# Who makes the low parts of the key/value filler's weights in the layers' attention: GpSimd, or VectorE in pairs

## The chip, the core and the metric

The kernel runs on one core of a Trainium2 chip. The time is device microseconds from start to end of the one launch. The core has TensorE (PE) for matrix products, VectorE (DVE) and ScalarE (ACT) for element work, GpSimd (POOL) for element work and powers, and SyncE (SP), which issues most DMAs. The engines run their own instruction streams and meet by semaphores.

## What is computed

Two transformer layers of one kind, then one block of another, on 256 rows of width 1024. What bears on this change is the attention of the two layers, and a projection of the last block that is computed beside it:

```python
for l in range(DEPTH):                       # DEPTH = 2, the "layers"
    proj = h @ w_in[l]                       # q, k, v of 8 + 8 heads, 2 + 2 key/value heads
    oa = global_attention(qa, ka, va)
    ob = window_sink_attention(qb, kb, vb, sink[l], slopes)
    mix = jnp.concatenate([rms(oa), rms(ob)], axis=-1) @ w_o[l]
    h = layer_norm(ALPHA * h + mix, ...)
    ...                                      # a PEER feed-forward, layer norm
# second block, cross attention:
mn = rmsnorm(mem, norm_mem)                  # depends on inputs alone
kx, vx = jnp.split(mn @ w_kv_x, 2, axis=-1)  # 1024 x 2048 weights
```

`mem` is an input, so `mn @ w_kv_x` can be computed at any time. The kernel does it inside the layers' attention, the keys in layer 0 and the values in layer 1.

## The kernel before

Large products are made in three passes for precision. Each weight is split into a high part `wh` (fp32r, a reduced form of fp32) and a low part `wl = w - wh`, and so are the activations (`xh`, `xl`); the product is xh·wh + xl·wh + xh·wl. Weights come in chunks of 1 MB, `[128, 2048]` fp32, into a ring of two slots (`ring[:, s, :]`). A chunk has four quarters of 128x512. For each quarter ScalarE copies the high part (`high`, L1405, signals `high_ready[q]`), and either GpSimd (`low`, L510) or VectorE (`low`, L2084) subtracts it to make the low part (signals `parts_ready[q]`); then TensorE multiplies, and signals `parts_free[q]`. When the last low part of a chunk is done, `chunk_free[s]` reaches 2, and SyncE issues the load of the next chunk into that slot. SyncE issues strictly in the order in which its program is written.

The attention of a layer is 8 units (a quarter of 8 heads' queries in each of two row tiles; units 0 to 3 are the windowed kind with sink, 4 to 7 the global kind). Per unit, TensorE makes scores, VectorE takes the maximum (`first`, L2160 or L2163 to L2170), ScalarE the exponentials (L1511), TensorE turns the probabilities (L688), ScalarE takes them out of PSUM (L1457), TensorE multiplies by the values (L971), and VectorE divides (`finish`, L2275 to L2294). VectorE's order per unit u is: scores of u + 2, `late(u - 1)`, wait for the values of u, `finish(u)`. `late` (L2301 to L2310) scales finished heads by a power that GpSimd makes (L496) after `finish` asked for it. `own` makes an engine wait for its own last write.

The **filler** is the key/value product: 4 chunks of 4 quarters, 16 quarters, two per unit. TensorE's order in unit u is: scores of u + 2, filler quarter 2u (`kv_quarter`, L1038), turned probabilities of u + 1, filler quarter 2u + 1, values of u. ScalarE makes a pair of high parts per unit 1 to 6 (`kv_high`), for quarters 4 to 15 (the first chunk's are made before the attention), and every second unit takes a finished filler chunk out of PSUM (`kv_done`, L1582) into the buffer `kvo`, which SyncE saves to DRAM (L354); from the second chunk on `kv_done` first waits until the save before it has landed (`kv_saved`), and its end lets TensorE begin the next filler chunk (`kv_free`). The chunks' low parts are GpSimd's (`kv_lows`, L594 to L606): after its rotation of the queries it makes 12 of them in six pairs, with the powers in between. The first chunk's four low parts are made by GpSimd (L566) and VectorE, two each. In SyncE's program the load of the fourth filler chunk stands ahead of the save of the first, and that load waits for slot 1 of the ring.

After the attention TensorE turns `o_all` (`to_xT`, L720) in two row tiles; for the second it waits for VectorE's last scaling. Before that it runs 14 dummy matmuls (L694).

Of the kernel before, what the change touches and what calls it, by code (L numbers as in the profile page):

```python
# [19 lines left out]
QW = CHUNK // 4  # L20
# [22 lines left out]
def build(nc, A, out):  # L43
# [4 lines left out]
    with ctx:  # L48
# [3 lines left out]
        def sem(name):  # L52
            return ctx.enter_context(nc.semaphore(name))
# [142 lines left out]
        mem_in = sem("mem_in")  # L196
        mem_used = sem("mem_used")
        memvar_ready, memrstd_ready = sem("memvar_ready"), sem("memrstd_ready")
        kv_begun = sem("kv_begun")
        kv_full, kv_free = sem("kv_full"), sem("kv_free")  # L200
        kv_out, kv_saved, kv_in = sem("kv_out"), sem("kv_saved"), sem("kv_in")
        memgain_in = sem("memgain_in")
# [269 lines left out]
        def _(pool):  # L472
            def own(ins):
                ins.then_inc(pool_own, 1)
                pool.wait_ge(pool_own, 1)
                pool.sem_inc(pool_own, -1)
# [15 lines left out]
            def power(n, at=0):  # L492

                pool.wait_ge(var_ready, 1)
                pool.sem_inc(var_ready, -1)  # L495
                pool.tensor_tensor(rstd[:, at:at + n], ve[:, at:at + n], mhalf[:, :].to_broadcast([P, n]),  # L496
                                   ALU.pow).then_inc(rstd_ready, 1)
# [8 lines left out]
            def low(s, q, parts=3):  # L506

                pool.wait_ge(high_ready[q], 1)
                pool.sem_inc(high_ready[q], -1)  # L509
                part = pool.tensor_tensor(wl[:, q, :], ring[:, s, q * QW:(q + 1) * QW],  # L510
                                          wh[:, q, :].bitcast(F32), SUB)
                if q < parts - 1:
                    part.then_inc(parts_ready[q], 1)
                else:
                    own(part)
                    pool.sem_inc(parts_ready[q], 1)
                    pool.sem_inc(chunk_free[s], parts - 2)
# [18 lines left out]
            for l in range(DEPTH):  # L536
# [56 lines left out]
                                           .to_broadcast([P, 10, HD]), MUL))  # L593
                pool.sem_inc(rotated_ready, 1)  # L594

                def kv_lows(s, q0):
                    for q in (q0, q0 + 1):
                        pool.wait_ge(high_ready[q], 1)
                        pool.sem_inc(high_ready[q], -1)
                        part = pool.tensor_tensor(wl[:, q, :], ring[:, s, q * QW:(q + 1) * QW],  # L600
                                                  wh[:, q, :].bitcast(F32), SUB)
                        if q < 3:
                            part.then_inc(parts_ready[q], 1)
                        else:
                            own(part)
                            pool.sem_inc(parts_ready[3], 1)  # L606
                            pool.sem_inc(chunk_free[s], 2)

                kv_lows(1, 0)
                pool.wait_ge(kv_begun, 1)  # L610
                pool.sem_inc(kv_begun, -1)
                kv_lows(1, 2)
                kv_lows(0, 0)
                power(16)
                kv_lows(0, 2)
                kv_lows(1, 0)
                power(4, 16)
                power(4, 24)
                kv_lows(1, 2)
                power(4, 20)  # L620
                low(0, 0)
                power(4, 28)
                low(0, 1)
# [1207 lines left out]
        def _(dve):  # L1831
# [248 lines left out]
            def low(s, q, freed=1):  # L2080

                dve.wait_ge(high_ready[q], 1)
                dve.sem_inc(high_ready[q], -1)  # L2083
                part = dve.tensor_tensor(wl[:, q, :], ring[:, s, q * QW:(q + 1) * QW],  # L2084
                                         wh[:, q, :].bitcast(F32), SUB)
                if q < 3:
                    part.then_inc(parts_ready[q], 1)
                else:
                    own(part)
                    dve.sem_inc(parts_ready[3], 1)  # L2090
                    dve.sem_inc(chunk_free[s], freed)
# [28 lines left out]
                                          xh[:, part, t * P:(t + 1) * P].bitcast(F32), SUB  # L2120
                                          ).then_inc(slot_free[2 + t] if i else xl_half[t], 1)

            def attention(units, first, finish, before=None, late=None, second=None):

                def scores(u):
                    s = u % 2
                    dve.wait_ge(dve_full[s], 1)
                    dve.sem_inc(dve_full[s], -1)
                    first(u, s)

                scores(0)
                if before:
                    before()
                scores(1)
                if second:
                    second()
                for u in range(units):
                    if u + 2 < units:
                        scores(u + 2)
                    if late:  # L2140
                        late(u - 1)
                    dve.wait_ge(dve_full[3], 1)
                    dve.sem_inc(dve_full[3], -1)
                    finish(u, 3)
                if late:
                    late(units - 1)
# [39 lines left out]
            for l in range(DEPTH):  # L2186
# [70 lines left out]
                def kv_lows():  # L2257
                    low(0, 2)
                    low(0, 3)
                    dve.sem_inc(kv_begun, 1)  # L2260

                def first(u, s):
                    ab, g, t = 1 - u // 4, u // 2 % 2, u % 2
# [49 lines left out]

                dve.wait_ge(gain_in[2], 16)
                dve.sem_inc(gain_in[2], -16)
                attention(8, first, finish, mem_lows, late, kv_lows)
                dve.sem_inc(gain_free[1], 1)
                halves_low_xT()
                low(0, 3)
# [720 lines left out]
```

## Time and profile before

| | |
|---|---|
| time, median of 3 runs | 2522.37 us (2522.11 to 2525.31) |
| the profiled execution | 2519.75 us, span 2517.1 us |
| TensorE busy | 2411.9 us, 96% |
| VectorE busy | 1747.7 us, 69% |
| ScalarE busy | 1344.4 us, 53% |
| GpSimd busy | 709.3 us, 28% |
| low parts of the filler on GpSimd (L600) | 24, at 83.2 to 1126.9 us |
| attention, layer 0, first scores to last values | about 60 to 129 us |
| attention, layer 1 | about 1069 to 1132 us |

How to read it: the busy times are shares of the whole span and say which engine sets the pace on the whole. What the change is worth must be read in the two attention stages, 5% of the span, from what each engine waits for there. In the rows "idle before <- X" is the time an engine sat idle before the instruction, and what ended it; "POOLq L599" and the like mean the engine's own sequencer, at a wait on that line.

### The profile page before, as it was taken

The page shows a single profiled execution, that of the slowest core. Times are in us where ns is not written, and L with a number is a line of the kernel's source. Part 1 is how long each engine was busy: PE and PEld are TensorE (multiplying, and loading weights), DVE is VectorE, ACT ScalarE, POOL GpSimd, SP SyncE. Part 2 cuts the span into 40 slices and gives each one's busy share as a digit, 9 for nine tenths or more (in the row PEclk, how much of TensorE's full clock was granted, in tenths as well). Part 3 has the DMA queues.
Part 4 walks back from the last instruction along what each step waited for, and adds up shares of the span by engine and source line. Part 5 has one row for each costly group of instructions (what it writes and reads, how often), then busy time and mean ns, then how long its engine had stood idle before and what let it go on. Part 6 is the DMA issues. An engine that isn't in the chain of part 4 may idle for free. (4 is left out here: it accounts for less than half of the span.)

```text
span 2517.1 us, 57290 instructions
## 1 busy us (share of the span) xinstructions
PE 2411.9 (96%) x16475; PEld 2207.7 (88%) x16475; DVE 1747.7 (69%) x3905; ACT 1344.4 (53%) x2396; POOL 709.3 (28%) x564
## 2 busy tenths in 40 slices
PE   7899999999999999989999999999999998899998
PEld 6789999999888888888999999988888887688996
DVE  5647777887777777564777788767777767455346
ACT  3545555776655555454455567655555543344443
POOL 5665444000000000556544400000000053144665
PEclk9999999999999999999999999999999998999999
DMA  6244566444566666624466644556666644433554
GB/s 240 79 156 157 211 221 224 170 160 171 185 236 246 238 241 240 239 79 140 167 210 227 228 164 151 180 176 247 236 243 239 245 156 155 141 134 110 177 183 149
DMA packets 98051, 475.27 MB, mean 189 GB/s; under 512 B 11809, under 2 KB 13345, under 8 KB 50721
## 3 DMA queue, kind: packets, MB, share of 16 engines
q1 hardware_dynamic: 97392, 472.91, 53.0%
q10 hardware_dynamic: 560, 1.19, 0.1%
q8 instruction: 44, 0.72, 0.1%
q14 instruction: 55, 0.44, 0.1%
HBM read 438.41 MB, written 35.65 MB: 188 GB/s over the span
## 5 line engine op out<-in xcount | busy, mean ns | idle before, releaser
L1405 ACT ACTIVATE wh<-ring 128x512 fp32r<-128x512 f32 x1428 | 882.7, 627 | 610.9 <-ACTq L1404 607.7
L2084 DVE TENSOR_TENSOR wl<-ring,wh 128x512 fp32r<-128x512 f32 x961 | 675.4, 708 | 268.4 <-DVEq L2083 250.7
L1093 PE MATMUL PS<-xh,wh 128*128 128x256 f32 x2048 | 593.4, 290 | 8.3 <-PEq L1089 6.3
L1093 PE MATMUL PS<-xl,wh 128*128 128x256 f32 x2048 | 579.2, 283 | 0.0
L1093 PE MATMUL PS<-xh,wl 128*128 128x256 f32 x2048 | 579.0, 283 | 0.0
L510 POOL TENSOR_TENSOR wl<-ring,wh 128x512 fp32r<-128x512 f32 x295 | 392.8, 1353 | 289.9 <-POOLq L509 286.7
L889 PE MATMUL PS<-wh,xh 128*128 128x512 f32 x1088 | 425.1, 391 | 2.3 <-PEq L886 2.1
L889 PE MATMUL PS<-wh,xl 128*128 128x512 f32 x1088 | 423.4, 389 | 0.0
L889 PE MATMUL PS<-wl,xh 128*128 128x512 f32 x1088 | 423.3, 389 | 0.0
L1093 PEld LDWEIGHTS PS<-xh,wh 128*128 128x128 f32 x2048 | 392.0, 191 | 15.3 <-issue 14.7
L1093 PEld LDWEIGHTS PS<-xl,wh 128*128 128x128 f32 x2048 | 392.6, 192 | 0.0
L1093 PEld LDWEIGHTS PS<-xh,wl 128*128 128x128 f32 x2048 | 392.0, 191 | 0.0
L496 POOL TENSOR_TENSOR rstd<-ve,mhalf 128x1 f32<-128x1 f32 (+3 forms) x30 | 30.2, 1007 | 1243.0 <-POOLq L495 1222.9
L636 POOL TENSOR_TENSOR wl<-ring,wh 128x512 fp32r<-128x512 f32 x144 | 205.5, 1429 | 230.3 <-POOLq L635 229.9
L889 PEld LDWEIGHTS PS<-wh,xh 128*128 128x128 f32 x1088 | 204.2, 188 | 48.8 <-issue 6.8
L889 PEld LDWEIGHTS PS<-wh,xl 128*128 128x128 f32 x1088 | 204.2, 188 | 42.8
L889 PEld LDWEIGHTS PS<-wl,xh 128*128 128x128 f32 x1088 | 204.3, 188 | 42.4 <-issue 0.5
L864 PE MATMUL PS<-xh,wh 128*128 128x256 f32 x688 | 196.7, 286 | 8.7 <-PEq L860 8.7
L864 PE MATMUL PS<-xl,wh 128*128 128x256 f32 x688 | 194.6, 283 | 0.0
L864 PE MATMUL PS<-xh,wl 128*128 128x256 f32 x688 | 194.5, 283 | 0.0
L1626 ACT ACTIVATE stg<-PS 128x256 f32<-128x256 f32 x256 | 97.9, 382 | 155.1 <-ACTq L1621 92.3
L1692 ACT ACTIVATE xh<-gains 128x256 fp32r<-128x256 f32 x248 | 103.5, 417 | 131.4 <-ACTq L1690 130.0
(338 smaller groups left out, 3813.0 us busy)
## 6 DMA issues: line engine op xcount, KB each, us to landing
ring<-in_peer_u SPq DMA_DIRECT2D x128, 1024.0 KB, 4.8
ring<-in_peer_v SPq DMA_DIRECT2D x128, 1024.0 KB, 4.8
acts<-stg SPq DMA_DIRECT2D x124, 256.0 KB, 2.1
gains<-acts SPq DMA_DIRECT2D x124, 256.0 KB, 4.8
ring<-in_w_in SPq DMA_DIRECT2D x24, 1024.0 KB, 4.9
ring<-in_w_gate_up SPq DMA_DIRECT2D x22, 1024.0 KB, 4.8
ring<-in_peer_wq SPq DMA_DIRECT2D x16, 1024.0 KB, 4.8
ring<-in_w_down SPq DMA_DIRECT2D x11, 1024.0 KB, 4.8
```

The costliest lines, as they stand in the source:

```text
L496: pool.tensor_tensor(rstd[:, at:at + n], ve[:, at:at + n], mhalf[:, :].to_broadcast([P, n]), ALU.pow).then_inc(rstd_ready, 1)
L510: part = pool.tensor_tensor(wl[:, q, :], ring[:, s, q * QW:(q + 1) * QW], wh[:, q, :].bitcast(F32), SUB)
L636: pool.tensor_tensor(wl[:, q, :], ring[:, s, q * QW:(q + 1) * QW], wh[:, q, :].bitcast(F32), SUB).then_inc(parts_ready[q] if q == 0 else p ...
L864: last = pe.matmul(PS[:, 2 * s + b, 0:S], w[:, q, k * CW + b * P:k * CW + (b + 1) * P], x[:, 2 * q + k, :], start=q + k + i == 0, stop=q + ...
L889: last = pe.matmul(acc[:, t, c * 512:(c + 1) * 512], wst[x][:, j, t * P:(t + 1) * P], w[:, q, :], start=begin and j + i == 0, stop=False)
L1093: last = pe.matmul(PS[:, 2 * j, 0:S], w[:, q, k * P:(k + 1) * P], x[:, at, :], start=at + i == 0, stop=at + i == 9)
L1405: act.activation(wh[:, q, :], ring[:, s, q * QW:(q + 1) * QW], ACT.Copy).then_inc(high_ready[q], 1)
L1626: last = act.activation(stg[:, s, j * S:(j + 1) * S], PS[:, 2 * j, 0:S], ACT.Gelu)
L1692: act.activation(wst[0][:, j, :], buf[:, j * S:(j + 1) * S], ACT.Copy).then_inc(cast_ready[j], 1)
L2084: part = dve.tensor_tensor(wl[:, q, :], ring[:, s, q * QW:(q + 1) * QW], wh[:, q, :].bitcast(F32), SUB)
```

## The change

The 12 low parts of each layer's filler go from GpSimd to VectorE. VectorE makes a pair in each of the units 1 to 6, after the scores of unit u + 2 and `late(u - 1)` and before it waits for unit u's values. GpSimd keeps only the powers in this stretch; before its next own low part (`low(0, 0)`, of the chunk that follows) it waits once for `kv_lows_done`, which VectorE gives in unit 6. The semaphore `kv_begun` goes. The arithmetic is the same.

```diff
@@ GpSimd @@
-                def kv_lows(s, q0):
-                    for q in (q0, q0 + 1):
-                        pool.wait_ge(high_ready[q], 1)
-                        pool.sem_inc(high_ready[q], -1)
-                        part = pool.tensor_tensor(wl[:, q, :], ring[:, s, q * QW:(q + 1) * QW],
-                                                  wh[:, q, :].bitcast(F32), SUB)
-                        if q < 3:
-                            part.then_inc(parts_ready[q], 1)
-                        else:
-                            own(part)
-                            pool.sem_inc(parts_ready[3], 1)
-                            pool.sem_inc(chunk_free[s], 2)
-
-                kv_lows(1, 0)
-                pool.wait_ge(kv_begun, 1)
-                pool.sem_inc(kv_begun, -1)
-                kv_lows(1, 2)
-                kv_lows(0, 0)
                 power(16)
-                kv_lows(0, 2)
-                kv_lows(1, 0)
                 power(4, 16)
                 power(4, 24)
-                kv_lows(1, 2)
                 power(4, 20)
+                pool.wait_ge(kv_lows_done, 1)
+                pool.sem_inc(kv_lows_done, -1)
                 low(0, 0)
                 power(4, 28)
@@ VectorE, attention @@
                     if late:
                         late(u - 1)
+                    if beside:
+                        beside(u)
                     dve.wait_ge(dve_full[3], 1)
                     dve.sem_inc(dve_full[3], -1)
                     finish(u, 3)
@@ VectorE @@
                 def kv_lows():
                     low(0, 2)
                     low(0, 3)
-                    dve.sem_inc(kv_begun, 1)
+
+                def kv_pair(u):
+
+                    if 0 < u < 7:
+                        s, q = (u + 1) // 2 % 2, 2 * (1 - u % 2)
+                        low(s, q)
+                        low(s, q + 1, 2)
+                    if u == 6:
+                        dve.sem_inc(kv_lows_done, 1)
...
-                attention(8, first, finish, mem_lows, late, kv_lows)
+                attention(8, first, finish, mem_lows, late, kv_lows, kv_pair)
```

## Rows read from the trace of the kernel before

**Rows 1.** The page, part 1: busy time, share of the span, instructions.
```profile
PE 2411.9 (96%) x16475; PEld 2207.7 (88%) x16475; DVE 1747.7 (69%) x3905; ACT 1344.4 (53%) x2396; POOL 709.3 (28%) x564
```

**Rows 2.** TensorE's waits, 64 to 134, then 1068 to 1138: total, times, longest.
```profile
PE PS L688 <- PEq L685: 7.8, 5, 2.7
...
PE PS L688 <- PEq L685: 6.7, 3, 3.7
```

**Rows 3.** Windows: length, busy of PE, PEld, DVE, ACT, POOL, clock, DMA.
```profile
68.00:73.00 5.00, 3.83 (x17) 2.71 (x18) 4.47 (x6) 1.99 (x5) 4.64 (x8) 0.66 0.01 5
...
118.00:123.00 5.00, 3.32 (x31) 3.15 (x29) 2.98 (x8) 3.75 (x7) 1.93 (x2) 1.00 0.02 6
```

**Rows 4.** Low parts and late scalings by line: count, ns min/median/max, first and last start.
```profile
L600 POOL TENSOR_TENSOR wl<-ring,wh x24: 1267/1288/1747, 83.2 to 1126.9; 128x512 fp32r<-128x512 f32 x24
...
L2084 DVE TENSOR_TENSOR wl<-ring,wh x961: 673/692/1839, 22.7 to 2504.6; 128x512 fp32r<-128x512 f32 x193
...
L2310 DVE TENSOR_TENSOR arena<-arena,rstd x8: 424/900/1394, 117.9 to 1137.1; 128x256 f32<-128x256 f32 x8
```

**Rows 5.** Timeline of GpSimd, layer 0: start, duration, instruction, idle before it.
```profile
91.77 2.51 POOL L600 TENSOR_TENSOR wl<-ring,wh 128x512 fp32r<-128x512 f32 x2 [5.88 <-POOLq L599]
...
109.70 2.98 POOL L600 TENSOR_TENSOR wl<-ring,wh 128x512 fp32r<-128x512 f32 x2
```

**Rows 6.** Timeline of TensorE, layer 0.
```profile
87.75 0.36 PE L1038 MATMUL PS<-xh,wh 128*128 128x256 f32 x1
...
90.10 1.06 PE L688 MATMUL PS<-ident,arena 128*128 128x128 f32 x8 [0.68 <-PEq L685]
...
99.21 1.06 PE L688 MATMUL PS<-ident,arena 128*128 128x128 f32 x8 [1.32 <-PEq L685]
...
120.05 1.06 PE L688 MATMUL PS<-ident,arena 128*128 128x128 f32 x8 [1.68 <-PEq L685]
...
135.00 1.06 PE L720 MATMUL PS<-ident,arena 128*128 128x128 f32 x8 [0.54 <-PEq L718]
```

**Rows 7.** Timeline of VectorE, layer 0.
```profile
83.65 1.09 DVE L2288 TENSOR_TENSOR arena<-arena 128x256 f32<-128x256 f32 x1
...
96.93 0.17 DVE L2161 TENSOR_SCALAR arena<-arena 128x4 f32<-128x4 f32 x1
...
103.69 0.16 DVE L2275 TENSOR_TENSOR arena<-PS,arena 128x4 f32<-128x4 f32 x1 [2.34 <-DVEq L2274]
...
109.88 3.35 DVE L2305 TENSOR_TENSOR arena<-arena,rstd 128x512 f32<-128x512 f32 x2 [1.72 <-DVEq L2301]
...
114.13 0.55 DVE L2285 TENSOR_TENSOR arena<-arena 128x256 f32<-128x256 f32 x1 [0.24 <-DVEq L1836]
...
115.16 0.93 DVE L2288 TENSOR_TENSOR arena<-arena 128x256 f32<-128x256 f32 x1
...
122.22 1.38 DVE L2310 TENSOR_TENSOR arena<-arena,rstd 128x256 f32<-128x256 f32 x1 [1.33 <-DVEq L2301]
...
124.42 0.18 DVE L2278 RECIPROCAL arena<-PS 128x4 f32<-128x4 f32 x1 [0.82 <-DVEq L2143]
...
129.08 0.18 DVE L2278 RECIPROCAL arena<-PS 128x4 f32<-128x4 f32 x1 [0.26 <-DVEq L2143]
```

**Rows 8.** Timeline of VectorE, layer 1.
```profile
1100.57 0.17 DVE L2161 TENSOR_SCALAR arena<-arena 128x4 f32<-128x4 f32 x1
...
1107.34 0.16 DVE L2275 TENSOR_TENSOR arena<-PS,arena 128x4 f32<-128x4 f32 x1 [2.34 <-DVEq L2274]
```

**Rows 9.** SyncE's first two filler saves, layer 0; landing times of each alone.
```profile
95.01 8.18 SPq L354 DMA_DIRECT2D kvs<-arena  x2
...
DMA to landing us min/median/max: 5.6/5.6/5.6
...
DMA to landing us min/median/max: 2.0/2.0/2.0
```

**Rows 10.** Timeline of ScalarE, layer 0: the second filler chunk's copy.
```profile
101.98 0.60 ACT L1582 ACTIVATE arena<-PS 128x512 f32<-128x512 f32 x1 [0.56 <-ACTq L1581]
```

More of the change, by code:

```diff
@@ L198, in build @@
         memvar_ready, memrstd_ready = sem("memvar_ready"), sem("memrstd_ready")
-        kv_begun = sem("kv_begun")
+        kv_lows_done = sem("kv_lows_done")
         kv_full, kv_free = sem("kv_full"), sem("kv_free")
@@ L2121, in halves_low_xT, with attention @@
                                           ).then_inc(slot_free[2 + t] if i else xl_half[t], 1)
-            def attention(units, first, finish, before=None, late=None, second=None):
+            def attention(units, first, finish, before=None, late=None, second=None, beside=None):
                 def scores(u):
```

## The prediction, as it was put on record

> **What bounds the kernel now.** I read the page's first part, then TensorE's waits in the two attention stages, then the stages' windows, then each engine's order in time. TensorE is busy 96% of the span [rows 1], so only what lengthens or shortens TensorE's own sequence moves the end. In the attention stage of layer 0 it waits 7.8 us in five waits, in that of layer 1 6.7 us in three [rows 2], all at the transposes of a unit's probabilities (L688). The first wait of each stage, 2.67 and 3.71 us, lies before unit 1, and nothing of the change runs by then. What the change can touch is the rest. In layer 0 that is 5.1 us: one wait of 1.4 in unit 0, still too early, and then 0.68, 1.32 and 1.68 ahead of the transposes of units 3, 4 and 7 [rows 6]; in layer 1 it is 3.0 us, of the last two kinds. A stage's last wait, 0.54 us, is at the transposes of the second row tile after the attention, L720, and it follows VectorE's last scaling [rows 6, 7].
>
> VectorE is the engine that runs closest behind. Between the units it is idle only where it waits for the values of a unit (2.34, 0.82, 0.26 us) or for a power from GpSimd [rows 7].
>
> **What the change does, part by part.** *Removed from GpSimd:* 12 low parts per layer, 24 in all, median 1.29 us each [rows 4], and its wait for VectorE. They are off its path to anything but TensorE's filler quarters and the powers.
>
> *Added to VectorE:* the same 12 in six pairs, one pair in each of units 1 to 6, between the next scores and `finish(u)`. An undisturbed one takes 0.69 us (median of 961, minimum 0.67) [rows 4]. A pair is 1.38 us; those of units 2, 4 and 6 end with `own`, a wait for the engine's own write, which cost 0.24 ahead of L2285 [rows 7], so 1.62. Per layer 3 x 1.38 + 3 x 1.62 = 9.0 us more VectorE work.
>
> *Given back on VectorE:* while GpSimd runs a low part, a VectorE operation with both inputs in SBUF is held up. L2305 took 3.35 us for two of 128x512 beside GpSimd's pair at 109.70, where 0.69 each is the price of that size, so 1.97 are lost. L2310 took 1.38 at 122.22, and 0.42 at its least: 0.96 lost. In `finish(4)` L2288 took 0.93 for 0.41 and L2285 0.13 more: 0.64 lost. [rows 4, 5, 7] Together 3.6 us a layer. For L2305 the trace has no undisturbed row; its bounds are 2 x 0.69 and the 3.35 measured, and I take 1.38 because L2310, the same operation on half the columns, has 0.42 as its least.
> The Trainium skill (SBUF — State Buffer, "SBUF: two separate sides") says that the port pair shared by VectorE and GpSimd is an exclusive lock, taken also by a VectorE operation with two SBUF inputs against a GpSimd one that reads SBUF. The rows just named agree. By it nothing holds up VectorE's new low parts, since GpSimd's powers are its only work left there and VectorE waits for those; were it otherwise, rival C's price would be the one to take.
>
> *VectorE's order, as a shift s of its work against before.* In layer 0, the small op that ends unit 4's scores starts at 96.93 and ends at 97.10 [rows 7]. Unit 1's step moves that by -0.4. L2288 took 1.09 at 83.65 beside GpSimd's first pair, for 0.41 [rows 7], so unit 3's scores and exponentials now come 0.7 earlier; the filler quarter that began at 87.75 waits for VectorE's first low part until 88.15, and the transposes behind it, which had 0.68 us to wait at 90.10 [rows 6], start at 89.7. Pair 2 (1.62) and the 4.25 us of `finish(2)` and scores 5 (from 97.10 to 101.35, where the idle 2.34 ahead of 103.69 begins) bring it to 102.5, pair 3 (1.38) to 103.9. `finish(3)` began at 103.69 after an idle 2.34 [rows 7], so **s = +0.26**. In layer 1 the same op ends at 1100.74, without the early gain, and `finish(3)` began at 1107.34 [rows 8]: 1100.74 + 1.62 + 4.25 + 1.38 = 1108.0, **s = +0.7**. From there, layer 0 / layer 1:
> late(3) -1.97 and pair 4 +1.62: -0.09 / +0.34.
> finish(4) -0.64: -0.73 / -0.30, so unit 7's scores are worked earlier.
> Pair 5 +1.38: +0.65 / +1.08.
> late(5) -0.96, pair 6 +1.62, less the idle 0.82 ahead of `finish(6)` [rows 7]: +0.49 / +0.92.
> Idle 0.26 ahead of `finish(7)` [rows 7]: +0.23 / **+0.66** (in layer 1 all the gains and idle times are taken as in layer 0).
> `finish(7)`, the last power and late(7) then lead to TensorE's transposes at 135.00 [rows 6], which waited for them, so this is what reaches the end: **+0.23 + 0.66 = +0.9 us**. The code behind the stage is the same; it is TensorE's and shifts whole.
>
> *TensorE's order.* A filler quarter now needs VectorE's pair. For the quarter ahead of unit 4's transposes GpSimd's pair was done at 94.28 [rows 5]; VectorE has the first low part at 97.4, so the quarter runs from 97.5 to 99.0. It ended at 97.9 before, and then TensorE waited 1.32 us for the exponentials until 99.21 [rows 6], so the transposes come no later. The first low parts of pairs 4 and 5 come at 112.2 and 118.4, about 1.1 and 1.8 us behind the quarters' old starts. Those slips end at unit 7's transposes, which waited 1.68 until 120.05 [rows 6] and now get their exponentials about 0.5 earlier, because of s = -0.73. So TensorE's own order comes out between -0.2 and +0.5, inside VectorE's.
>
> *An added wait and what is queued behind it.* VectorE waits for ScalarE's high parts at each pair. GpSimd's starts show when these were there: 91.77 for pair 2, 109.70 at the latest for pair 4 [rows 5]; VectorE comes at 96.7 and 111.5. Nothing is lost there. `finish(u)` is queued behind it; it frees the value banks (slot 3), which TensorE wants over 2 us later each time. GpSimd's new wait for `kv_lows_done` has `low(0, 0)` and the last power behind it; VectorE gives it at about 125, and GpSimd gets there at 129.
>
> *SyncE's queue.* The last low part of pair 2 frees ring slot 1. Before, it came at 94.28, and SyncE issued the 1 MB load and, queued behind it, at 95.01, the save of the first filler chunk. That save took 5.6 us to land; the next one, with no load ahead, took 2.0 [rows 9]. It landed at 100.6; ScalarE's next copy into the same buffer started at 101.98 [rows 10]. Now slot 1 is freed at 98.3, the save lands at about 104.4 (layer 1: 1108.4), and ScalarE waits some 2.5 us. Behind the copy stand the exponentials of unit 5 and the release of the filler's bank. They slip by 1.5 to 1.9 us. TensorE would in any case have waited 1.2 to 1.5 for pair 4 soon after, and the rest falls into the 1.68 us ahead of unit 7. I cost it at nothing; that cover is thin (0.1 to 0.5 us).
> The Trainium skill (DMA: Bandwidth & Descriptors, "Queues, rings and completion order") says that a completion increment lands only after every earlier write of that DMA engine, so a small save cannot report before the 1 MB ahead of it. The 5.6 against 2.0 us agree.
>
> **Sum.** The profiled execution took 2519.75 us (span 2517.1); with +0.9 it is 2520.7. It lies 2.6 below the median of the three runs, so the predicted median is 2522.4 + 0.9 = **2523.3**.
>
> **Rivals.**
> (A) *The late save reaches the end.* If the cover above is missing, 1.5 and 1.85 us come on top of PE's order in the two layers: 2522.4 + 3.4 = 2525.8. For: 2.5 us of wait on ScalarE are close to certain. Against: unit 7's slack.
> (B) *Slower, by the clock.* Behind the 2.67 us wait the granted clock was 0.66 in 68 to 73; around the 1.68 us wait it stayed 1.00 [rows 3, 6]. If the wait for the filler's bank or for a pair grows from my 1.2 to 1.5 to well over 2 us, the matmuls behind it run at the lower of the two levels, 1.2 for 2.4 GHz: a mean of 0.66 over 5 us is 1.7 us of work lost. Once per layer, plus about 1.5 us of longer wait: 2 x 3.2 + 0.9 = 7.3, 2529.7. It decides from a wait somewhere between 1.7 and 2.7.
> (C) *VectorE becomes the bound in earnest.* L2305 stays slow by itself (+1.97), and a low part on VectorE costs 1.2, midway from the median to the maximum of 1.84 [rows 4], in the six that follow the last idle time of size (+3.0): about 5 a layer on top, 2 x 5 + 0.9, 2533.
> (D) *Faster.* All waits left to gain are 0.68 + 1.32 + 1.68 and 1.32 + 1.69 = 6.7 us; if the give-back outweighs the pairs by 1 to 2 us a layer, 2520. Over 5 us would take nearly all of them.
> (E) *The pairs block VectorE on ScalarE's high parts*, so that the work isn't where the change puts it. The margins of 5 and 2 us speak against it; it would give about +3, 2525.5.
>
> **How the numbers follow.** This kernel's measurement tells some 0.2% (5 us) from no change. Chances: forecast 0.62 (own range 2520.5 to 2526), A 0.14, B 0.06, C 0.06, D 0.08, E 0.04. All but B, C and a quarter of D lie within 5 us: faster by over 0.2% 0.02, within 0.88, slower 0.10 (B, C, rounded down). Range 2519.5 to 2528.5: from D, with the spread of the runs (2522.1 to 2525.3), to A with L2305's upper bound in one layer.
>
> **What the next profile shows.** Right: 12 more L-low parts of 0.69 us on VectorE per layer and L2305 near 0.69; ScalarE's copy at about 104.5 instead of 101.98 and SyncE's load at 98.7; small waits of TensorE at the filler quarters of units 3, 5, 6; both stages within 1.5 us of their length; the granted clock 1.00 behind unit 2. Wrong: a clock below 0.9 after unit 2, L2305 still at 1.7, or the stage over 2 us longer.

## The result and the profile after

The changed kernel took **2528.18 us** (median of 16 runs, 2523.42 to 2532.8) against 2525.05 us of the kernel before beside it (16 runs, 2520.61 to 2527.89): a ratio of **1.0016, interval 1.0009 to 1.0023**, that is 2.3 to 5.8 us slower (the two medians alone are 3.1 us apart). The forecast was +0.9 us (1.0004). The profiled execution took 2528.86 us, its span 2526.3.

The page, part 1, answers to [rows 1]:

```profile
PE 2415.6 (96%) x16475; PEld 2213.9 (88%) x16475; DVE 1756.1 (70%) x3929; ACT 1344.9 (53%) x2396; POOL 679.3 (27%) x540
```

The 24 low parts have gone from GpSimd to VectorE (x540 for 564, x3929 for 3905). VectorE is busy 8.4 us longer, GpSimd 30.0 less. TensorE has the same instructions and 3.7 us more busy time: some ran slower.

TensorE's waits in the two attention stages, 64 to 141 and 1068 to 1147 (total, times, longest), against [rows 2]:

```profile
PE PS L669 <- PEq L666: 5.6, 3, 3.0
PE PS L1019 <- PEq L1011: 4.5, 2, 2.9
...
PE PS L669 <- PEq L666: 5.0, 3, 3.7
PE PS L1019 <- PEq L1011: 4.7, 2, 3.1
```

The waits at the transposes (L669, before L688) are shorter than before. A new pair stands at the filler quarters (L1019). TensorE's timeline of layer 0 from unit 4's scores on (start, duration, instruction, idle before it) answers to [rows 6]:

```profile
97.56 2.00 PE L914 MATMUL PS<-arena 64*128 64x256 f32 x16
...
101.21 0.35 PE L1019 MATMUL PS<-xh,wh 128*128 128x256 f32 x1 [1.66 <-PEq L1011]
...
106.84 1.13 PE L914 MATMUL PS<-arena 64*128 64x256 f32 x8
110.85 0.55 PE L1019 MATMUL PS<-xh,wh 128*128 128x256 f32 x1 [2.87 <-PEq L1011]
113.55 1.25 PE L669 MATMUL PS<-ident,arena 128*128 128x128 f32 x8
...
126.48 1.06 PE L669 MATMUL PS<-ident,arena 128*128 128x128 f32 x8 [0.29 <-PEq L666]
...
141.44 0.74 PE L701 MATMUL PS<-ident,arena 128*128 128x128 f32 x5 [0.54 <-PEq L699]
```

Three things are to be seen. The quarter ahead of unit 4's transposes waits 1.66 for VectorE's pair, which takes the place of the 1.32 for the exponentials. The quarter ahead of unit 5's, number 8, the first of the third filler chunk, waits **2.87** us (3.06 in layer 1), and its first product then takes 0.55 for 0.36: the twelve run from 110.85 to 113.55, 2.70 us for an ordinary 1.54. And the 1.68 us ahead of unit 7's transposes have shrunk to 0.29, so 1.4 of the slip was taken up there. The windows from 108 to 118 (columns as in [rows 3]) show the clock:

```profile
108.00:113.00 5.00, 2.15 (x10) 2.19 (x11) 3.14 (x7) 2.46 (x6) 2.40 (x1) 0.76 0.14 53
113.00:118.00 5.00, 5.00 (x42) 4.93 (x41) 2.50 (x4) 3.50 (x8) 0.51 (x1) 0.90 0.19 29
```

Before, the granted clock of both windows was 1.00. ScalarE and SyncE say what quarter 8 waited for (against [rows 10] and [rows 9]): ScalarE's copy of the second filler chunk, behind which its exponentials stand; SyncE's load and save; and the save's landing time:

```profile
109.84 0.60 ACT L1563 ACTIVATE arena<-PS 128x512 f32<-128x512 f32 x1 [4.93 <-ACTq L1562]
110.79 1.57 ACT L1492 ACTIVATE arena<-PS,arena 128x256 f32<-128x256 f32 x4 [0.35 <-ACTq L1487]
```
```profile
102.00 0.33 SPq L325 DMA_DIRECT2D ring<-in_w_kv_x  x1
102.43 0.37 SPq L354 DMA_DIRECT2D kvs<-arena  x1
```
```profile
DMA to landing us min/median/max: 7.3/7.3/7.3
```

The first save was issued at 102.43 and landed (its completion was signalled) at 109.7; the copy, which overwrites what is being saved, began at 109.84, having waited 4.93 us (4.85 in layer 1). It frees the bank that quarter 8 fills.

VectorE's timeline of layer 0 (against [rows 7]):

```profile
100.37 1.29 DVE L2065 TENSOR_TENSOR wl<-ring,wh 128x512 fp32r<-128x512 f32 x2
...
113.65 1.29 DVE L2296 TENSOR_TENSOR arena<-arena,rstd 128x512 f32<-128x512 f32 x2 [1.72 <-DVEq L2292]
...
118.12 0.18 DVE L2269 RECIPROCAL arena<-PS 128x4 f32<-128x4 f32 x1 [1.97 <-DVEq L2126]
...
124.86 0.18 DVE L2269 RECIPROCAL arena<-PS 128x4 f32<-128x4 f32 x1 [0.97 <-DVEq L2126]
...
128.83 0.42 DVE L2301 TENSOR_TENSOR arena<-arena,rstd 128x256 f32<-128x256 f32 x1 [1.33 <-DVEq L2292]
```

A pair takes 1.29 us. L2296 takes 1.29 where L2305 took 3.35, and L2301 at 128.83 takes 0.42 for the 1.38 of its counterpart at 122.22: the give-back came in full. VectorE waits 1.97 and 0.97 us for values, so here, where the save is late, it is not what bounds the stage.

**The measure used below.** One layer's *stretch* is the time from the start of unit 4's scores (94.26 before, 97.56 after, in layer 0) to the start of the last transposes (135.00, 141.44). It holds all that the late load and the pairs from unit 3 on can do, and not what differs from one execution to the next ahead of it: from the second unit's scores (65.37 before, 67.19 after) to unit 4's, layer 0 took 28.9 us before and 30.4 after, but 28.0 to 29.5 in the twelve other executions, with either order of work. "Landing" is the time from the save's issue to its completion. Every stretch is read from the one profiled execution of its row, every ratio from all executions. Layer 0 / layer 1, in us:

| kernel | stretch | first save's landing | longest wait within | ratio (interval) |
|---|---|---|---|---|
| before | 40.74 / 40.76 | 5.6 / 5.4 | 1.68 / 1.69 | |
| after | 43.88 / 43.69 | 7.3 / 7.2 | 2.87 / 3.06 | 1.0016 (1.0009 to 1.0023) |
| a1, after, save first | 40.98 / 40.98 | 2.0 / 2.0 | 1.66 / 1.66 | 1.0009 (1.0000 to 1.0018) |
| a2, before, save first | 40.73 / 40.76 | 2.0 / 2.0 | 1.66 / 1.68 | 1.0000 (0.9991 to 1.0009) |
| a3, before, late load | 44.05 / 42.58 | 6.8 / 5.4 | 3.10 / 2.02 | 1.0035 (1.0022 to 1.0047) |
| a4, pairs 1, 2 on GpSimd | 41.62 / 40.69 | 5.4 / 5.5 | 1.85 / 1.32 | 1.0000 (0.9991 to 1.0009) |
| b1, after again | 43.55 / 45.20 | 7.1 / 7.4 | 2.63 / 3.27 | 1.0002 (0.9993 to 1.0012) |
| b2, after, kept busy | 42.88 / 41.83 | 7.3 / 5.9 | 1.66 / 1.66 | 1.0004 (0.9995 to 1.0013) |
| c1, pairs in idle time | 39.39 / 39.11 | 5.5 / 5.5 | 1.32 / 1.32 | 0.9984 (0.9975 to 0.9993) |
| c2, c1 and save first | 39.35 / 39.08 | 2.0 / 2.0 | 1.32 / 1.32 | 0.9982 (0.9973 to 0.9991) |
| d1, before, 16 more waits | 40.88 / 40.74 | 5.7 / 5.4 | 1.80 / 1.66 | 1.0000 (0.9991 to 1.0009) |
| d2, after, 104 more waits | 41.36 / 41.57 | 5.7 / 5.9 | 1.66 / 1.82 | 1.0003 (0.9994 to 1.0012) |
| d3, c2 again | 39.36 / 39.09 | 2.0 / 2.0 | 1.32 / 1.32 | 0.9984 (0.9975 to 0.9993) |
| d4, after, third time | 43.79 / 42.77 | 7.3 / 5.9 | 2.83 / 1.85 | 1.0012 (1.0003 to 1.0021) |

By its stretches the change costs 3.14 + 2.93 = 6.1 us, most of the difference of the two profiled spans (9.2). The ratios say less: the same changed kernel gave 1.0016, 1.0002 (b1) and 1.0012 (d4). One thing that blurs them is in the traces: from the last transposes of layer 1 to the end, where no edit changes the work, the 14 profiled executions took between 1375.4 and 1384.2 us. That spread is larger than any difference of the stretches, so below the stretches carry the argument and the ratios only bound it.

### The profile page after: what moved, and what is told of

Its sections match the earlier page's. It is cut to its first block and busy times, and to the rows that moved or that the text cites. A ratio compares the mean times of both kernels' runs of the same rounds, so it can differ in the third digit from the quotient of the medians.

```text
span 2526.3 us, 57290 instructions
## 1 busy us (share of the span) xinstructions
PE 2415.6 (96%) x16475; PEld 2213.9 (88%) x16475; DVE 1756.1 (70%) x3929; ACT 1344.9 (53%) x2396; POOL 679.3 (27%) x540
## 5 line engine op out<-in xcount | busy, mean ns | idle before, releaser
L2065 DVE TENSOR_TENSOR wl<-ring,wh 128x512 fp32r<-128x512 f32 x985 | 687.3, 704 | 267.6 <-DVEq L2064 251.1
```

## The experiments

### Is it the save behind the late load?

The two kernels with SyncE's save ahead of the second load; nothing else is changed:

```diff
-                for c in range(2):
-                    load(A["w_kv_x_2"][N_KV * l + 2 + c], c)
-                for c in range(2):
-                    save_kv(c)
+                load(A["w_kv_x_2"][N_KV * l + 2], 0)
+                save_kv(0)
+                load(A["w_kv_x_2"][N_KV * l + 3], 1)
+                save_kv(1)
```

On the changed kernel (a1):

> The changed kernel, with one edit in SyncE's program: the save of the first filler chunk is issued before the load of the fourth, not behind it. Theory 1 (the late save): the save of the first chunk now lands long before ScalarE's second copy (by the changed kernel's trace it was ready at about 90 us and nothing but the load's wait for slot 1 held it), TensorE's waits of 2.9 and 3.1 us ahead of filler quarter 8 and the clock that falls behind them go, and the time falls by 3 to 6 us from the changed kernel's, to a ratio of 0.9990 to 1.0005 to before. Theory 2 (VectorE's pairs are late for TensorE and VectorE has become the bound): the ratio stays at 1.0016, and filler quarter 8 still starts late.

On the kernel before (a2):

> The kernel before, with the same edit in SyncE's program. It is the control. In the kernel before the save landed 1.1 us ahead of its need in layer 0, so both theories expect a ratio of 1.000, within 0.0005.

SyncE of a1, layer 0, and the first save's landing:

```profile
87.20 0.33 SPq L354 DMA_DIRECT2D kvs<-arena  x1
99.34 0.33 SPq L325 DMA_DIRECT2D ring<-in_w_kv_x  x1
```
```profile
DMA to landing us min/median/max: 2.0/2.0/2.0
```

TensorE of a1 over the same stretch:

```profile
94.89 2.00 PE L914 MATMUL PS<-arena 64*128 64x256 f32 x16
98.55 0.36 PE L1019 MATMUL PS<-xh,wh 128*128 128x256 f32 x1 [1.66 <-PEq L1011]
...
113.04 0.36 PE L1019 MATMUL PS<-xh,wh 128*128 128x256 f32 x1 [1.00 <-PEq L1011]
119.26 0.36 PE L1019 MATMUL PS<-xh,wh 128*128 128x256 f32 x1 [0.51 <-PEq L1011]
...
135.87 1.06 PE L701 MATMUL PS<-ident,arena 128*128 128x128 f32 x8 [0.56 <-PEq L699]
```

The load is as late as in the changed kernel (4.45 us behind the start of unit 4's scores, 4.44 there, 0.32 before), but the save no longer stands behind it. The wait at quarter 8 is gone; what stays are waits of 1.0 and 0.5 for VectorE's pairs, which unit 7 absorbs. The stretches are 40.98 and 40.98, +0.24 and +0.22 over before. a2 is the kernel before to 0.01 us. So 2.9 of the 3.1 us of layer 0 and 2.7 of the 2.9 of layer 1 come through the save, and the moved work itself costs 0.2. The ratios don't show this: a1's 1.0009 lies above the 0.9990 to 1.0005 that was expected, and among the three of the changed kernel.

### Is the late load enough by itself?

The kernel before, GpSimd's low parts and all, with the second load held until `finish(2)` (a3):

```diff
-                for c in range(2):
-                    load(A["w_kv_x_2"][N_KV * l + 2 + c], c)
+                load(A["w_kv_x_2"][N_KV * l + 2], 0)
+                sp.wait_ge(kv_late, 1)
+                sp.sem_inc(kv_late, -1)
+                load(A["w_kv_x_2"][N_KV * l + 3], 1)
...
+                    if u == 2:
+                        dve.sem_inc(kv_late, 1)
```

> The kernel before, GpSimd making all its low parts as ever, but SyncE holds the load of the fourth filler chunk (and with it the save queued behind it) until VectorE is in the middle of finish(2), about where the changed kernel frees slot 1. Theory 1: this alone costs what the change cost, 3 to 6 us, ratio 1.0012 to 1.0024, with ScalarE waiting 3 to 5 us for the landed save and TensorE about 3 us ahead of filler quarter 8. Theory 2: no low part is late and VectorE has no more work, so the ratio is 1.000.

TensorE's waits in layer 0's stretch:

```profile
PE PS L1041 <- PEq L1033: 3.1, 1, 3.1
PE PS L691 <- PEq L688: 1.6, 2, 1.3
PE PS L723 <- PEq L721: 0.5, 1, 0.5
```

The wait at quarter 8 appears without any change to VectorE or GpSimd: 3.10 and 2.02 us, and the stretches grow by 3.3 and 1.8. Its ratio of 1.0035 (8.8 us, above the 1.0012 to 1.0024 that was expected) is more than these 5.1. In its profile some 5.7 us more than before lie behind the attention of layer 1, which this edit doesn't touch. I have no cause for them; that part took 1384.2 us here, against 1375.4 to 1383.0 in the others.

The other way round, the changed kernel with the lows of the second filler chunk (pairs 1 and 2) given back to GpSimd, so that slot 1 is freed early again (a4; SyncE's program is the original one):

```diff
+                for q in range(4):
+                    if q == 2:
+                        pool.wait_ge(kv_begun, 1)
+                        pool.sem_inc(kv_begun, -1)
...
+                    part = pool.tensor_tensor(wl[:, q, :], ring[:, 1, q * QW:(q + 1) * QW],
+                                              wh[:, q, :].bitcast(F32), SUB)
...
-                    if 0 < u < 7:
+                    if 2 < u < 7:
```

> The changed kernel with the second filler chunk's two pairs (units 1 and 2) back on GpSimd, so that slot 1 is freed as early as before; VectorE keeps the pairs of units 3 to 6. Theory 1: the whole loss goes, and what VectorE gains from GpSimd's silence in late(3), finish(4) and late(5) stays: ratio 0.9985 to 1.0000. Theory 2: only the first two of six pairs stop costing, and VectorE still has four: ratio 1.0008 to 1.0012.

The save goes out 0.77 us behind the start of unit 4's scores and lands in 5.4; layer 1's stretch is 40.69, 0.07 below before, layer 0's is 0.9 longer, with a last wait of 1.85 for 0.54 that layer 1 doesn't have. VectorE and GpSimd show where that comes from:

```profile
130.32 1.51 DVE L2317 TENSOR_TENSOR arena<-arena,rstd 128x256 f32<-128x256 f32 x1 [1.33 <-DVEq L2308]
```
```profile
130.25 1.30 POOL L511 TENSOR_TENSOR wl<-ring,wh 128x512 fp32r<-128x512 f32 x1
```

GpSimd's first low part of the next product starts 0.07 us ahead of VectorE's last scaling but one, which then takes 1.51 us. In layer 1 it starts 0.27 us behind that scaling (1136.75 against 1136.48), which takes 0.42; in a1 0.28 behind it (130.18 against 129.90), with 0.43. So that loss is one of how GpSimd's and VectorE's work happen to meet, not of the save. Four pairs on VectorE cost nothing in layer 1. With a1 and a3 this says that the two pairs that free slot 1 late are what the change loses by.

### How much of it is the clock?

Three products that nobody reads keep TensorE busy ahead of quarter 8 (b2), beside the changed kernel run again (b1):

```diff
+                    if i == 8:
+                        pe.wait_ge(slot_free[2], 1)
+                        for _ in range(3):
+                            pe.matmul(PS[:, 4, :], ident[:, :], h[:, 0, 0:512], start=True, stop=True)
                     if q == 0:
                         pe.wait_ge(kv_free, 1)
```

> The changed kernel once more, on the same chip as the three below, and for a second look at its trace. Theory 1 (the late save is the whole cost of the change) expects TensorE's two waits of about 3 us ahead of filler quarter 8 again, the stretch from unit 4's scores to the last transposes of the attention at 43.7 to 43.9 us in each layer (40.7 before), and a ratio of 1.0012 to 1.0024. Open: in the two layers of the first trace the save took 7.3 and 7.2 us to land, 5.4 to 5.6 in the kernel before. If it is 5.5 here in a layer, that layer's stretch is 42 us.

> The changed kernel with three dummy products (2.7 us) on TensorE ahead of filler quarter 8, into a bank that is free. ScalarE still waits for the save, and the quarter still starts when the copy is out. Theory 1 with the clock: of the 3.1 and 2.9 us that a layer lost, the later start is about 1.9 and the lower clock behind the wait 1.1 (12 filler products in 2.7 us for 1.5). With the dummies the granted clock stays 1.00 there, the quarter takes 1.5 us, and a layer gets back 1.1: stretch 42.6 us, ratio 1.0006 to 1.0014. If the clock has no part, the stretch stays at 43.8.

b2's windows from 103 on (quarter 8 begins at 108.87):

```profile
103.00:108.00 5.00, 5.00 (x31) 3.56 (x31) 4.17 (x10) 0.14 (x1) 0.00 (x0) 1.00 0.48 187
108.00:113.00 5.00, 4.67 (x34) 3.74 (x32) 2.98 (x7) 4.19 (x9) 2.90 (x1) 1.00 0.14 52
```

The save landed as late in layer 0 as in the changed kernel (7.3), but the clock stayed at its upper level, and the stretch is 42.88: 0.7 to 1.0 less than the three executions of the changed kernel with that landing (43.55 to 43.88). In layer 1 the landing was 5.9, so its 41.83 is not to be held against them. A second comparison needs no dummies: in layer 1 d4 and d2 (both below) had landings of 5.95 and 5.91 us and waits of 1.85 and 1.82, but in d4 the clock fell to its lower level (0.50 from 1115.0 to 1118.4) and in d2 it stayed at 1.00; the stretches are 42.77 and 41.57, 1.2 apart. So the clock's part is about 1 us in layer 0; in b1's layer 1 it was more, since quarter 8, the transposes and the quarter behind them all ran slow. The medians don't resolve it: 1.0002 and 1.0004, both below what was expected (1.0012 to 1.0024, 1.0006 to 1.0014). b1's own ratio is also below what its stretches say (+7.3 us, 0.3%); its profiled execution, 2529.99 us, was the third slowest of 12 with a median of 2526.94, and how late the save landed in the others isn't known.

### Why did the save take 7.3 us in place of 5.6?

DMA packets of the two executions: first the changed kernel from 107.5 to 108.4 (the rate in 40 equal slices, by the packets' starts; their number; share of each queue), then from 108.55 to 109.1:

```profile
GB/s 273 0 91 0 91 0 91 0 0 0 728 0 0 0 0 0 0 0 0 0 0 0 0 0 0 0 0 0 0 0 0 0 0 0 0 0 0 0 0 0
DMA packets 11, 0.03 MB, mean 32 GB/s; under 512 B 4, under 2 KB 4, under 8 KB 10
...
q8 instruction: 1, 0.02, 6.7%
q1 hardware_dynamic: 10, 0.01, 3.8%
...
DMA packets 2, 0.00 MB, mean 4 GB/s; under 512 B 1, under 2 KB 1, under 8 KB 2
...
q1 hardware_dynamic: 2, 0.00, 2.9%
```

and the kernel before, from 100.3 to 101.6:

```profile
DMA packets 1, 0.02 MB, mean 13 GB/s; under 512 B 0, under 2 KB 0, under 8 KB 0
...
q8 instruction: 1, 0.02, 4.6%
```

Queue q8 carries, by its label, instructions, 16 KB a packet, and this one takes 0.96 us. In the kernel before it comes 5.5 us behind the save's issue, when no packet of the save is left. In the changed kernel it comes 5.3 us behind (the 728 of slice 11, at 107.7). The ten packets of q1 in this window start ahead of it, none starts behind it until 108.4, and the last two start only at 108.7, a microsecond after it. The same straggler, a packet of the save that starts 0.9 to 1.0 us behind the start of one of q8 (in three cases with a last one 1.1 to 1.2 behind), stands in all six cases with a landing of 7.1 or more (after and b1 in both layers, b2 and d4 in layer 0) and in none of those with 5.4 to 5.9. In a3, with 6.8, the packet of q8 falls in the midst of the load, and the save's last packets end at 6.4 us behind its issue in place of 5.0 to 5.5. Position alone doesn't decide it: q8's packet came 5.06 to 5.35 us behind the issue in the six late landings of 7.1 or more, but also 5.28 in d2's layer 0, 5.17 in b2's layer 1 and 4.98 in d4's layer 1, where the save landed in 5.7 to 5.9. What else decides it stays open; the trace doesn't say which DMA engine a packet ran on. Nor does the straggler explain the whole delay: in the six cases the save's last packet ended 6.0 to 6.5 us behind the issue and the landing followed 0.8 to 1.1 us later, in the short ones 0.3 to 0.5. To move the packet, I put more instructions on TensorE's queue at the very start, where it is idle until 15.4 us:

```diff
-            pe.wait_ge(consts_pe, 1)
+            for _ in range(17):
+                pe.wait_ge(consts_pe, 1)
```

(17 in d1, on the kernel before; 105 in d2, on the changed one.) The distances of 3.4 to 4.4 us in the two texts are 1.8 us too small, all alike: I had misread the zero of the packet times.

> The kernel before, with 16 more instructions on TensorE's queue at the very start (its first wait repeated, while TensorE is idle until 15.4 us anyway), so that every later 16 KB packet of the instruction queue q8 comes about 0.8 to 1.0 us earlier beside the work. In the kernel before that packet starts 3.7 us (layer 0) and 4.4 us (layer 1) behind the issue of unit 0's save, when the save's last packets have gone, and the save lands in 5.6 and 5.4 us. In the kernel after it starts 3.4 us behind the issue and the save lands in 7.3 and 7.2 us. Theory (a packet of instructions among the save's last packets holds one of the 16 DMA engines for its 0.96 us, and the landing with it): layer 0's packet now starts at 2.7 to 2.9 us and the first save lands in 6.6 to 7.3 us, layer 1's at 3.4 to 3.6, on the edge, landing 5.4 or about 7.2; the stretch from unit 4's scores to the last transposes goes from 40.74 us to 41 to 42.3 where the save is late. Rival (landing depends on what VectorE or TensorE do beside it): landings of 5.4 to 5.6 us and stretches of 40.7 as before. Time within 0.2% by either.

> The changed kernel with 104 more instructions on TensorE's queue at the very start, while it is idle: the packets of q8 come 5 to 6 us earlier beside the work, ahead of the load in front of unit 0's save. Theory (packet of instructions among the save's): the save lands in 5.4 to 5.6 us in both layers in place of 7.2 to 7.3, the wait before quarter 8 falls from 2.9 and 3.1 us to 1.2 to 1.4, the clock stays at its upper level there, and the stretch from unit 4's scores to the last transposes is 41.3 to 42.3 us in place of 43.9 and 43.7: 1.5 to 2.5 us saved in each layer. Rival (the landing's 7.2 us belong to the changed work): stretches of 43.5 to 45 as before.

> The changed kernel once more, on the same chip as the three others, to hold beside them: its first comparison gave 1.0016, its second 1.0002. By the stretches of its traces (2.8 to 4.4 us more in a layer than before, two layers) it should be 1.0005 to 1.0025.

d1 missed: the packet of layer 0 came 6.0 us behind the save's issue, later rather than earlier, so the landing of 5.7 tests nothing. In d2 layer 1's packet was gone from the save's neighbourhood, and layer 0's had hardly moved (5.3) but had no packet of the save behind it. Landings were 5.7 and 5.9, where 5.4 to 5.6 was expected. Whether the added instructions did that in layer 0 or chance did, can't be told; d4, the changed kernel unaltered, also landed at 5.9 once in layer 1. What d2 does give is the changed kernel with its late load and a landing of the size that I had reckoned with. TensorE, layer 0, and the windows from 103 on:

```profile
95.05 2.00 PE L914 MATMUL PS<-arena 64*128 64x256 f32 x16
98.70 0.35 PE L1020 MATMUL PS<-xh,wh 128*128 128x256 f32 x1 [1.66 <-PEq L1012]
104.34 1.14 PE L914 MATMUL PS<-arena 64*128 64x256 f32 x8
106.80 0.36 PE L1020 MATMUL PS<-xh,wh 128*128 128x256 f32 x1 [1.32 <-PEq L1012]
...
136.41 0.85 PE L701 MATMUL PS<-ident,arena 128*128 128x128 f32 x6 [0.54 <-PEq L699]
```
```profile
103.00:108.00 5.00, 3.68 (x31) 3.20 (x31) 4.02 (x12) 1.86 (x5) 0.00 (x0) 1.00 0.46 179
108.00:113.00 5.00, 4.74 (x42) 4.50 (x43) 3.13 (x6) 4.11 (x9) 2.91 (x1) 1.00 0.04 13
```

Quarter 8 waits 1.32 (1.82 in layer 1), the clock stays at 1.00, and the stretches are 41.36 and 41.57: +0.6 and +0.8 over before, not +3.1 and +2.9. d4 on the same chip took 1.0012 with one late landing, d2 1.0003 with none.

### A version that beats both

In the changed kernel VectorE is idle for 4.59 us ahead of unit 4's scores (98.85), and for 1.72 and 1.33 ahead of the scalings at 113.65 and 128.83, where it waits for a power. c1 puts the pair of unit 2 ahead of `scores(u + 2)`, those of 4 and 6 ahead of `late(u - 1)`, into these three, and leaves the odd ones where the change put them. c2 has the save first as well; d3 is c2 once more:

```diff
                 for u in range(units):
+                    if beside and u == 2:
+                        beside(u)
                     if u + 2 < units:
                         scores(u + 2)
+                    if beside and u in (4, 6):
+                        beside(u)
                     if late:
                         late(u - 1)
-                    if beside:
+                    if beside and u % 2:
                         beside(u)
```

> The changed kernel with three of VectorE's six pairs moved into waits that its trace shows: the pair of unit 2 ahead of the scores of unit 4 (4.6 us idle there), those of units 4 and 6 ahead of late, where VectorE waits 1.7 and 1.3 us for a power. SyncE's order stays. Theory 1: slot 1 is freed some 5 us earlier and the save lands at 100 to 102, about when it is needed, TensorE's waits ahead of quarters 6, 8 and 10 go, and unit 7's scores come 2 us earlier, so that the 1.68 us wait of the kernel before goes too: stretch 39.0 to 39.8 us (40.7 before), ratio 0.9985 to 0.9995. Rival (VectorE's 9 us of added work cost what they cost wherever they stand): ratio above 1.0005.

> The same, with the save of the first filler chunk issued before the load of the fourth. Theory 1: if the save of the kernel above lands after its need in a layer, this one is faster there by that, otherwise equal: stretch 39.0 to 39.3 us in both layers, ratio 0.9985 to 0.9993. Rival as above: above 1.0005.

> The kernel with the save ahead of the load and VectorE's pairs of units 2, 4 and 6 in its idle time, run again unchanged: ratio 0.9975 to 0.9990 once more, stretches of 39.1 to 39.4 us. If the first result was chance of the chip, 1.000.

TensorE of c2, layer 0:

```profile
95.82 2.00 PE L914 MATMUL PS<-arena 64*128 64x256 f32 x16
100.77 1.06 PE L669 MATMUL PS<-ident,arena 128*128 128x128 f32 x8 [1.32 <-PEq L666]
...
120.21 1.06 PE L669 MATMUL PS<-ident,arena 128*128 128x128 f32 x8 [0.29 <-PEq L666]
...
135.17 1.06 PE L701 MATMUL PS<-ident,arena 128*128 128x128 f32 x8 [0.54 <-PEq L699]
```

No filler quarter of the stretch waits any more, and the wait ahead of unit 7 has gone from 1.68 to 0.29. The stretches are 39.1 to 39.4, 1.4 to 1.7 below the kernel before, three times over, and the ratios 0.9984, 0.9982 and 0.9984 (a shade below the 0.9985 that was the lowest expected for c1 and c2) with upper ends of 0.9991 to 0.9993. Against a1, which has the save first as well but the pairs where the change put them, c2's stretches are 1.6 and 1.9 us shorter: that is the placement alone. In c1 slot 1 is freed so early that the save goes out 0.7 us ahead of unit 4's scores (94.75), so that a load in front of it does no harm; putting the save first then adds nothing that can be measured.

## Why the prediction was wrong, step by step

**The step that failed** is the last term, "SyncE's queue": "I cost it at nothing; that cover is thin (0.1 to 0.5 us)". The mechanism was there as it was put: the load waits for VectorE's last low part of pair 2, the save stands behind the load, ScalarE's copy behind the save, and quarter 8 behind that. The distance of the save from unit 4's scores was right too: 4.84 us forecast (99.1 less 94.26), 4.87 measured. Three sizes were off.
- *The landing.* I took 5.3 to 5.6 us from one row [rows 9], the only one there was. Of the ten landings in the five executions with the changed order of work and the save behind the load (after, b1, b2, d2, d4) six were 7.1 to 7.4 and four 5.7 to 5.9. So ScalarE waited 4.93 us, not 2.5 (3.38 in d2).
- *The cover.* Even with a landing of 5.7 and 5.9 (d2) the late save cost 0.4 and 0.6 us over a1. That is a quarter to a third of what rival A put on a layer (1.5 and 1.85), and not my "nothing". With the late landing the loss passed A's price.
- *The clock.* Rival B made the condition right, "between 1.7 and 2.7": waits of 1.32 and 1.82 (d2) kept 1.00, of two of 1.85 one kept it (a4) and one lost it (d4), and 2.02 (a3) and those of 2.63 to 3.27 all lost it. I gave B 0.06 because I set its wait by the same single landing. B is also not a rival to A but what A turns into: the late landing made both. Two of the prediction's own signs of being wrong came, a clock below 0.9 after unit 2 (0.76 from 108 to 113) and a stage over 2 us longer.

The sum in layer 0: 0.24 for VectorE's order, 0.38 for a late save that lands in time (41.36 less 40.98), 2.5 for the late landing and the clock behind it (43.88 less 41.36), of which the clock's part is about 1. In layer 1: 0.22, 0.59 and 2.1.

**VectorE's order** was right in kind: in a1, without the late save, VectorE no longer waits for values ahead of `finish(5)` and `finish(7)`, and it is TensorE that waits for VectorE's pairs. The size came out by luck as well: +0.23 forecast for layer 0, +0.24 measured (a1), +0.66 against +0.22 for layer 1. In a1's layer 0 `finish(7)` starts 35.36 us behind unit 4's scores, 34.82 before, so +0.54 and not +0.23; a pair took 1.29 for 1.38, but the idle time behind those that end with `own` was 0.44 to 0.56 where 0.24 was reckoned. Then 0.29 came back because L2276 took 0.54 at 131.23, where L2285 had taken 0.83, both beside a low part of GpSimd that now lies a little otherwise; I hadn't reckoned with that. The give-back on L2305 (1.97 forecast, 2.06 measured) and L2310 (0.96, 0.96) came as worked out. The Trainium skill's exclusive port pair (SBUF — State Buffer, "SBUF: two separate sides") agrees with the same rows: with GpSimd's low parts gone, 1.29 for two where it was 3.35.

**TensorE's small waits** were right, where the save did not disturb (a1). By their distance from unit 4's scores, the quarters of pairs 4 and 5 began 1.3 and 1.9 us later than before (1.1 and 1.8 forecast), and unit 7's transposes only 0.1 later. The quarter ahead of unit 4's transposes began 3.66 us behind them where 3.2 was forecast (97.5 less 94.26), so these came 0.2 late, not in time.

**Rivals C and E** are refuted: a pair takes 1.29 us and L2296 1.29, and none of the five pairs in the stretch starts behind an idle time. **D**, a gain, was not in the change but in its neighbourhood (c1, c2).

The range, 2519.5 to 2528.5, held with luck: 2528.18 lies 0.3 us inside it, and 2.7 of the 4.9 us between it and the forecast 2523.3 come from the kernel before, whose median over 16 runs was 2525.05 and not 2522.4. "Within 0.2%" held. The change itself was forecast some four times too small.

## What to carry to other kernels

When an operation moves to another engine, follow which buffer its last read frees and what is queued behind the transfer that waits for that buffer, and issue a small transfer that somebody waits for ahead of a large one that nobody waits for yet: here the moved work cost 0.2 us a layer, the save behind the late load 2.7 to 2.9. A landing time read from one row is a draw and not a constant; put a larger one through the sum as well, and look at what the clock did behind waits of that length elsewhere in the trace. Put added work into the receiving engine's idle rows: the same six pairs, three of them moved by a few lines, turned ratios of 1.0016, 1.0002 and 1.0012 into 0.9984, 0.9982 and 0.9984.

## What the runs showed of the hardware

- A 256 KB save took 2.0 us to land alone (a1, a2, c2, d3), and 5.4 to 7.4 with a 1 MB load issued 0.44 us ahead of it. The Trainium skill (DMA: Bandwidth & Descriptors, "Queues, rings and completion order") says that a completion shows only when all earlier writes of that DMA engine are done; the runs agree but don't isolate it: in the kernel before the save's own first packet starts only at 99.1 us, with the load's last at 99.2, so its data stood in line too. Some 1.5 us of the longest landings came where a packet of q8 had fallen among the save's last.
- A 16 KB packet of queue q8 took 0.93 to 1.2 us beside these saves. In six of six landings of 7.1 us or more a late packet of the save began 0.9 to 1.0 us behind the start of one; in three others, where q8's packet came at a like distance, none did and the save landed in 5.7 to 5.9 us. This is read from the packets; no experiment isolated it.
- The order in which VectorE and GpSimd start decided the price by a hair: VectorE's scaling of 128x256 took 1.51 us when GpSimd's low part had started 0.07 us ahead of it, and 0.42 to 0.43 when that started 0.27 to 0.28 us behind (a4, a1).
- TensorE's granted clock was still 1.00 behind waits of 1.32, 1.66, 1.80 and 1.82 us within a busy stretch, and behind one of 1.85 (a4). At another of 1.85 (d4), at 2.02 (a3), and at 2.63 to 3.27 (after, b1, d4, a3) it fell to its lower level: 0.50 from 1115.0 to 1118.4 in d4, from 110.6 to 114.0 in the changed kernel. Three products in the gap kept it at 1.00 (b2, layer 0).
